# Two pairs of heads share one rounding and one low part of their attention values

## What is computed

```python
y_a = conv_module(a_val, a_gate, conv_w, conv_b, conv_g, conv_beta)
y_b = forgetting_attention(heads(bq), heads(bk), heads(bv), bf, f_bias)
y_c = dilated_attention(rope(heads(cq)) * HEAD_DIM ** -0.5, rope(heads(ck)), heads(cv))
y = jnp.concatenate([y_a, merge(y_b), merge(y_c)], axis=-1)
return y @ w_o
# in each head: p = softmax(q k^T + mask); o = p v
```

## Time and profile before

| | us |
|---|---|
| median of 3 runs | 962.61 (962.4 to 962.81) |
| the profiled execution | 962.67 |
| its span in the trace | 960.9 |

### The profile page before, as it was taken

One profiled execution on the slowest core, in us unless ns is written; L12 is line 12 of the kernel. 1 busy time (PEld: TensorE's weight loads), 2 busy tenths in 40 slices (PEclk: granted clock), 3 DMA queues, 4 the chain that ended last, 5 costly groups with the idle time before them and its releaser, 6 DMA issues.

```text
span 960.9 us, 14786 instructions
## 1 busy us (share of the span) xinstructions
PE 951.9 (99%) x5284; PEld 812.3 (85%) x5284; DVE 656.0 (68%) x956; ACT 508.6 (53%) x691; POOL 46.6 (5%) x51
## 2 busy tenths in 40 slices
PE   9999999999999999999999999999999999999997
PEld 6888888899878888888888888888988788888886
DVE  5656656699998555656675565667999976565565
ACT  6554555445684554455455455545557655554541
POOL 0000000011102000000020000002001010000000
PEclk9999999999999999999999999999999999999999
DMA  9666566567525656566565655565765355655551
GB/s 321 241 214 211 175 209 227 188 219 222 163 88 181 213 176 217 175 197 234 175 214 175 217 176 194 194 223 174 246 207 154 126 194 175 209 184 182 197 190 44
DMA packets 127235, 185.48 MB, mean 193 GB/s; under 512 B 6264, under 2 KB 100608, under 8 KB 126432
## 3 DMA queue, kind: packets, MB, share of 16 engines
q1 hardware_dynamic: 123584, 178.91, 55.5%
q0 software_dynamic: 3472, 6.04, 2.7%
q10 hardware_dynamic: 144, 0.07, 0.0%
HBM read 181.83 MB, written 1.06 MB: 190 GB/s over the span
## 4 chain that ended last, share of the span: by engine, by line
PE 94%; DVE 3%; ACT 2%; issue 0%; DVEq 0%
PE bank L573 30%; PE bank L577 16%; PE ybank L535 9%; PE ybank L545 9%; PE ybank L541 9%; PE ybank L797 2%; PE ybank L801 2%; PE ybank L802 2%; PE bank L509 2%; PE bank L443 2%; PE bank L514 2%; PE bank L512 2%; PE bank L493 1%; DVE w_lo L1184 1%; PE ybank L509 1%; PE ybank L512 1%
## 5 line engine op out<-in xcount | busy, mean ns | idle before, releaser
L1184 DVE TENSOR_TENSOR w_lo<-raw,w_hi 128x2048 fp32r<-128x2048 f32 x154 | 352.8, 2291 | 234.9 <-ACT w_hi L944 234.9
L573 PE MATMUL bank<-xT,w_hi 128*128 128x512 f32 x1280 | 446.3, 393 | 0.0
L944 ACT ACTIVATE w_hi<-raw 128x2048 fp32r<-128x2048 f32 (+1 forms) x159 | 303.8, 1911 | 253.8 <-PE bank L577 112.1
L577 PE MATMUL bank<-xT,w_lo 128*128 128x256 f32 x1280 | 359.7, 281 | 0.0
L573 PEld LDWEIGHTS bank<-xT,w_hi 128*128 128x128 f32 x1280 | 240.3, 188 | 52.5
L577 PEld LDWEIGHTS bank<-xT,w_lo 128*128 128x128 f32 x1280 | 241.3, 189 | 1.6
L535 PE MATMUL ybank<-w_hi,yT_hi 128*128 128x512 f32 x416 | 165.7, 398 | 0.0
L545 PE MATMUL ybank<-w_hi,yT_lo 128*128 128x512 f32 x416 | 163.2, 392 | 0.0
L541 PE MATMUL ybank<-w_lo,yT_hi 128*128 128x512 f32 x416 | 162.4, 390 | 0.0
L545 PEld LDWEIGHTS ybank<-w_hi,yT_lo 128*128 128x128 f32 x416 | 77.9, 187 | 18.9 <-DVE yT_lo L1507 0.7
L535 PEld LDWEIGHTS ybank<-w_hi,yT_hi 128*128 128x128 f32 x416 | 78.3, 188 | 16.7 <-issue 1.2
(11 more groups left out here) (137 smaller groups left out, 858.4 us busy)
## 6 DMA issues: line engine op xcount, KB each, us to landing
raw<-in_ffn_in SPq DMA_DIRECT2D x170, 512.0 KB, 4.5
raw<-in_ffn_out SPq DMA_DIRECT2D x88, 512.0 KB, 4.0
raw<-in_w_in SPq DMA_DIRECT2D x40, 512.0 KB, 4.4
raw<-in_w_o SPq DMA_DIRECT2D x16, 512.0 KB, 4.1
gb<-in_ln_gb SPq DMA_DIRECT2D x6, 1024.0 KB, 7.1
raw<-in_ffn_in SPq DMA_DIRECT2D x12, 256.0 KB, 5.8
raw<-in_w_in SPq DMA_DIRECT2D x4, 520.0 KB, 7.3
qk_swap<-qk_raw POOLq DMA_DIRECT2D x16, 128.0 KB, 3.0
```

What stands on the lines that cost most here:

```text
L573: m = eng.matmul(dst[:, :], wh[:, k, g, cols], xT[:, kk, :, :].rearrange("p a n -> p (a n)"), start=kk == 0, stop=False, skip_group_check= ...
L577: m = eng.matmul(dst[:, SEQ:2 * SEQ], wl[:, k, g, cols], xT_hi[:, kk, :], start=False, stop=kk == KT - 1, skip_group_check=True)
L944: eng.activation(w_hi[:, s, 0:width], raw[:, s, 0:width], ACT.Copy).then_inc(hi_done, 1)
L1184: eng.tensor_tensor(w_lo[:, s, 0:width], raw[:, s, 0:width], w_hi[:, s, 0:width].bitcast(F32), ALU.subtract).then_inc(lo_done, 1)
```

## The change

The values of pairs 0 and 1 are computed one after the other at the end of step 2, and those of pairs 2 and 3 at the end of step 4. A table `Y_GROUP` says at which pair's turn which pairs are done. The second pair of each goes into columns 256 to 511 of bank 3. Then one ScalarE instruction rounds both (128 x 512), and one VectorE instruction subtracts both. Pairs 4 and 5 stay alone, in their own turn, pair 5 in the second half of the bank. Only even pairs wait for the low part before them, and only they set the start flag. `probT` has four buffers.

```diff
+Y_GROUP = {0: (), 1: (0, 1), 2: (), 3: (2, 3), 4: (4,), 5: (5,)}
...
-        probT = sb("probT", [P, 2, CAUSAL])
+        probT = sb("probT", [P, 4, CAUSAL])
...
+        def y_bank(pairs):
+
+            first = pairs[0] % 2 * SEQ
+            return bank[3][:, first:first + len(pairs) * SEQ].rearrange("p (k n) -> p k n", n=SEQ)
...
                 eng.wait_ge(pT_ready, count(pT_ready, l, 2 * p + 2))
-                if p > 0:
+                if p == 0:
+                    eng.wait_ge(sums_ready, count(sums_ready, l, 1))
+                elif p % 2 == 0:
 
                     eng.wait_ge(y_ready, count(y_ready, l, p))
-                else:
-                    eng.wait_ge(sums_ready, count(sums_ready, l, 1))
...
-                        m = eng.matmul(bank[3][i * HD:(i + 1) * HD, toks], v[:, t, (n + i) * HD:(n + i + 1) * HD],
-                                       probT[:, i, cols], start=t == 0, stop=t == 1)
+                        dst = bank[3][i * HD:(i + 1) * HD, p % 2 * SEQ:(p % 2 + 1) * SEQ]
+                        m = eng.matmul(dst[:, toks], v[:, t, (n + i) * HD:(n + i + 1) * HD],
+                                       probT[:, (2 * p + i) % 4, cols], start=t == p % 2 == 0, stop=t == 1,
+                                       skip_group_check=True)
...
                         if lagged and i == 3:
-                            values(l, SLOTS[s - 1][1])
+                            for p in Y_GROUP[SLOTS[s - 1][1]]:
+                                values(l, p)
...
-                    eng.activation(probT[:, i, :], bank[2][:, 0:CAUSAL], ACT.Copy).then_inc(pT_ready, 1)
+                    eng.activation(probT[:, (2 * p + i) % 4, :], bank[2][:, 0:CAUSAL], ACT.Copy).then_inc(pT_ready, 1)
...
-                    if lagged:
-                        pair = SLOTS[s - 1][1]
-
-                        eng.wait_ge(pv_done, count(pv_done, l, pair + 1))
-                        eng.activation(yT_hi[:, Y_KT[pair], :], bank[3][:, 0:SEQ], ACT.Copy).then_inc(y_hi_done, 1)
+                    if lagged and Y_GROUP[SLOTS[s - 1][1]]:
+                        pairs = Y_GROUP[SLOTS[s - 1][1]]
+                        k0, n = Y_KT[pairs[0]], len(pairs)
+
+                        eng.wait_ge(pv_done, count(pv_done, l, pairs[-1] + 1))
+                        eng.activation(yT_hi[:, k0:k0 + n, :], y_bank(pairs), ACT.Copy).then_inc(y_hi_done, n)
...
-                if s >= 2 and SLOTS[s - 2][0] == "pair":
-                    pair = SLOTS[s - 2][1]
-                    eng.wait_ge(y_hi_done, count(y_hi_done, l, pair + 1))
-                    eng.tensor_tensor(yT_lo[:, Y_KT[pair], :], bank[3][:, 0:SEQ], yT_hi[:, Y_KT[pair], :].bitcast(F32),
-                                      ALU.subtract).then_inc(y_ready, 1)
+                pairs = Y_GROUP[SLOTS[s - 2][1]] if s >= 2 and SLOTS[s - 2][0] == "pair" else ()
+                if pairs:
+                    k0, n = Y_KT[pairs[0]], len(pairs)
+                    eng.wait_ge(y_hi_done, count(y_hi_done, l, pairs[-1] + 1))
+                    eng.tensor_tensor(yT_lo[:, k0:k0 + n, :], y_bank(pairs), yT_hi[:, k0:k0 + n, :].bitcast(F32),
+                                      ALU.subtract).then_inc(y_ready, n)
```

## The result

The changed kernel takes 964.51 us (median of 17 runs), the kernel before in the same comparison 963.04 us: ratio 1.0016, 95% interval 1.0009 to 1.0022. In a second comparison it was 964.19 against 963.21, ratio 1.0010 (1.0001 to 1.0019). So it is slower by 1.0 to 1.5 us. I had forecast 962.9 against 962.61, 0.3 us slower, with a range up to 963.8. The direction was right, and so was the statement that 0.2% would not be exceeded; the size was not. Of the 1.6 us between 962.9 and 964.51, 0.4 is that the kernel before itself has a median of 963.04 over 17 executions, not the 962.61 of the three that I started from; the rest is the change.

The account below looks back on a forecast made before the run. TensorE, busy 951.9 of 960.9 us, was taken as the bound. Gains from grouping values were lost to waits, leaving 0.14 us per layer, 0.28 in all: 962.9 against 962.61, range 961.5 to 963.8.

Parts of the forecast that it names:

- Price of a group of values: On TensorE, a group costs 0.80 us; a second directly behind it 0.63, bounds 0.57 and 0.80.
- Steps 1 and 2: Pairs 0 and 1: scores of step 2 0.80 us earlier, next scores 0.17 earlier, masks unmoved, no wait for low part.
- Step 3: Next scores wait for ScalarE's fkT copy until 267.56; TensorE idle 0.83 us, net 0.14 earlier.
- Step 4: Probability copy 0.34 us earlier, pair 2's values start without wait at 272.01; next scores at 273.44, 0.29 later.
- Step 5: Second joined rounding starts 273.66; low part and masks 0.14 us later, passed on through VectorE, so the layer ends 0.14 later.
- Doubling one layer: Second layer's attention taken to repeat the first's pattern, so one layer's 0.14 us is counted twice.
- The sum: Two layers at 0.14 us give 0.28 on the profiled 962.67: 962.95; for the median 962.9.
- (a): Rival: idle time in step 3 halves TensorE's clock for one step, 5.3 us more per layer, 973.5; chance 0.03.
- (b): Rival: fqT/fkT copies less late, low part not delaying masks; 0.73 us gained per layer, 961.2, or half, 961.9; chance 0.20.
- (c): Rival: a second group in the same bank costs its full pitch or somewhat more, 963.0 to 963.4; chance 0.12.
- The range: 961.5 to 963.8 us: half of (b) below, (c) above, each with the 0.4 spread of three runs.

Follow-up runs that it names:

- fq_early: Changed kernel, but ScalarE copies fqT and fkT at the beginning of step 3; 964.42 us against 963.42 for the kernel before, ratio 1.0011.
- again: The changed kernel run once more, unaltered, for a second trace; 964.19 us against 963.21 for the kernel before, ratio 1.0010.
- only01: Changed kernel with only pairs 0 and 1 joined, pairs 2 and 3 in their own turns; 963.94 us against 963.21 for the kernel before, ratio 1.0007.
- split_late: Changed kernel, but in step 5 VectorE does the weight split behind both normalisations; 965.43 us against 963.42 for the kernel before, ratio 1.0011.
- narrow: Changed kernel, joined rounding and low part covering only the first pair (128x256), work left out; 962.92 us against 962.98 for the kernel before, ratio 0.9999.
- narrow_low: Changed kernel, rounding at full width, only the joined low part at half width; one execution 967.59 us, against 962.98 for the kernel before.
- singles: Changed kernel without the joining: each pair in its own turn with its own rounding and low part; 963.41 us against 963.21, ratio 1.0003.

## Why the prediction was wrong, step by step

- **Price of a group of values**: right. Two groups take 1.45 us (261.24 to 262.69) against 0.80 + 0.63 = 1.43. Scores of step 2 came 4.52 us after those of step 1 (4.51 forecast), those of step 3 10.47 (10.45).
- **Steps 1 and 2, masks of step 3 at 263.63 "where they start now"**: this is the term that was mis-sized. On the scale from the first scores I had them at 11.80; they came at 11.96. The rounding began 1.63 us after the values instead of 1.55 (260.85 to 262.40), took 0.60 instead of 0.57, and the low part followed 0.10 behind its end instead of 0.05. I had taken the hand-over from the rows of single pairs (257.26 behind 256.34) and the length from a copy of another tile. Three errors of 0.03 to 0.08 lie in series, with a reserve that I had myself called little. About 0.13 of the 0.16 are separate waits before the joined instructions (last section). The first fill that reads the low part, which I had without a wait, waited 0.19 for it (264.31). (A slip without effect: eight loads at 0.07 are 0.56, not 0.57.)
- **Step 3**: the mechanism was right, the scores of step 4 wait for the copy of fkT. With the masks 0.15 late the copy is 0.14 late, and TensorE followed it by 0.12, not 0.05: 15.94 instead of 15.73. I called this wait the place where the gain is lost. fq_early shows that it is not: with 1.0 us of it taken away the layer is 0.08 shorter.
- **Step 4**: right within 0.04. From the scores of step 4 to those of step 5 it is 5.92 us (268.16 to 274.08) against 5.88.
- **Step 5**: right in kind, wrong in size. The second rounding started at 22.04 instead of 21.83. Of this, 0.16 is the lateness of the masks of step 3, which I had left out of the later steps because I had put it at nothing: VectorE hands it on to the masks of step 4 (17.37 instead of 17.56 - 0.34 = 17.22), and these through the exponents to ScalarE's weight split (20.19 instead of 20.37 - 0.34 = 20.03). Behind the split the rounding could have started at 20.19 + 1.80 = 21.99; the values, again 1.63 us before it, held it 0.05 longer. Then it again had the longer way to the masks: 23.35 instead of 23.04, before 22.91. The transposes of step 6 waited for VectorE as forecast (0.49), 0.43 us later than before instead of 0.14. So the end of layer 1 carries 0.16 from the masks of step 3, 0.05 from the values and 0.09 from the length and the hand-over behind the second rounding that my sum lacked. The late scores of step 4 add next to nothing, as fq_early shows.
- **Doubling one layer**: wrong. Layer 2 costs 0.28 more, by the place of an instruction in ScalarE's program. No row of the kernel before shows that place: there ScalarE's rounding follows the weight split without idle time.
- **The sum**: 2 x 0.14 = 0.28 forecast, 0.44 + 0.71 = 1.15 in the traces. The missing 0.87 is 2 x 0.30 from the sizes above and 0.27 from layer 2. So the step that failed is the hand-over between engines around the joined rounding and low part, which I had priced like that of single pairs.
- **The rivals**: (a) did not come, the clock stays at 1.00 over a pause of 1.0 us of the matmul side, which says no more than that a pause of this length is harmless. (b), to which I gave 0.20, rested on the copies being less late and on the low part not delaying the masks; the scores of step 4 did wait for the copy of fkT, and the low part delays the masks more than I said. (c), a second group at full pitch, is refuted by the pitch of 1.45.
- **The range**: it took its upper end from the price of the second group and the spread of the runs. Even there the 0.17 of a dearer second group was put into step 5 alone (0.21 per layer), though in step 2 it would have made the masks of step 3 late as well. The serial hand-overs had no bounds at all, though they carried the sum, and the spread of three runs (0.4) was smaller than that of a larger number: the medians of the unchanged kernel went from 962.98 to 963.42.

## What to carry to other kernels

Joining two instructions saves their fixed cost but makes the first result wait for the second. Where the instruction lies in a chain between engines (values, rounding, low part, masks), the width is paid in full, and the saving counts only as far as it lies in the same chain. Here, from the masks of step 3 to those of step 5, 0.34 us went (the low part that VectorE no longer does in step 4), but 0.05 came before the second rounding, 0.30 between it and the low part, and 0.27 between low part and masks: 11.39 us instead of 11.10. When three engines are each nearly full in a stretch, idle time of the busiest is not by itself a price: take it away (as here, 1.0 us) and see what comes back (0.08). In a sum where a mere tenth decides, each hand-over between engines is a term with bounds of its own.

## What was not expected of the hardware

- A ScalarE instruction whose semaphore had been seen still started 0.33 us later at one place of the program, in all seven traces in which ScalarE stands idle before the rounding of pairs 0 and 1 and its program is not lengthened (changed, again, only01, fq_early, split_late, narrow, narrow_low), in layer 2 alone, and 0.04 with twelve more waits ahead. VectorE has one case of the same kind, in narrow_low alone: an instruction at 656.88 (L1294) stands 0.42 us behind its wait, and its idle time is 0.60 instead of the 0.23 of the same instruction in narrow, which has two more instructions at the start of VectorE's program. Both delays lie between a separate wait (next point) and its instruction. The cause is inferred, not shown.
- The low part starts 0.10 us behind the end of the joined rounding also where both are 256 wide (narrow: 263.48 to 263.58), and 0.03 behind it in the kernel before (257.64 to 257.67). The chain of work in order of time shows what lies between. First step 3 of the kernel before, then that of the changed kernel (DVEq is a wait that VectorE's sequencer does as an instruction of its own):

```profile
263.27 0.02 issue
263.30 0.42 DVE yT_lo L1446
...
263.48 0.03 issue
263.50 0.02 DVEq L1456
263.52 0.04 issue
263.57 0.69 DVE yT_lo L1457
```

Before the joined rounding stands one too (`ACTq L1161` above). Every trace with joined pairs has such a wait before each joined rounding and low part, the 256-wide ones of narrow included, and has it before none of the single ones. singles has none, though it reads the bank in the same form as narrow (258.36 to 258.39). What is left as the difference is that the joined instruction adds 2 to its semaphore instead of 1; no run changes this alone. An estimate from these rows: in the first group the two waits are worth 0.06 us at the rounding (from the start of the second pair's values 1.63 - 0.65 = 0.98 instead of 0.92) and 0.07 at the low part, in the second 0.05 (the split holds the rounding until then) and 0.07. That is 0.25 of the 0.30 us per layer that my sum lacked, if all of it reaches TensorE.
